# A two-layer hybrid decoder step: taps before each finish, no barrier behind the attention stream, row sums from the rows as loaded

## What is computed

```
h = x + W_out[ concat_g RMSNorm_g(mixer_g(RMSNorm(x))) ]
y = h + W2 relu(W1 RMSNorm(h))^2
```

```
def rmsnorm(x, g):
    xf = x.astype(jnp.float32)
    xf = xf * lax.rsqrt(jnp.mean(xf * xf, axis=-1, keepdims=True) + EPS)
    return xf.astype(x.dtype) * g

def merge_and_ffn(x, outs, p):
    B, T = x.shape[:2]
    o = jnp.concatenate([rmsnorm(o_i.reshape(B, T, GROUP_WIDTH), p['gnorm_g'][i])
                         for i, o_i in enumerate(outs)], axis=-1)
    h = x + o @ p['w_out']
    u = jax.nn.relu(rmsnorm(h, p['norm2_g']) @ p['w_ff1'])
    return h + jnp.square(u) @ p['w_ff2']
```

## Time and profile before

| | us |
|---|---|
| median of three runs | 3520.0 |
| the profiled execution, its own time | 3523.57 |
| its span, first to last instruction | 3521.8 |
| PE busy in it | 3298.5 (94%) |
| DVE busy | 1469.6 (42%) |
| ACT busy | 1017.1 (29%) |
| POOL busy | 203.7 (6%) |

### The profile page before, as it was taken

One profiled execution on the slowest core, in us unless ns is written; L12 is line 12 of the kernel. 1 busy time (PEld: TensorE's weight loads), 2 busy tenths in 40 slices (PEclk: granted clock), 3 DMA queues, 4 the chain that ended last, 5 costly groups with the idle time before them and its releaser, 6 DMA issues.

```text
span 3521.8 us, 55523 instructions
## 1 busy us (share of the span) xinstructions
PE 3298.5 (94%) x22450; PEld 1882.3 (53%) x22450; DVE 1469.6 (42%) x2767; ACT 1017.1 (29%) x1805; POOL 203.7 (6%) x136
## 2 busy tenths in 40 slices
PE   7999989888699999999999998888887999999998
PEld 4555466666444444444445555666664444444444
DVE  6865643333544311332178556433336533113322
ACT  2123344443433300231012232444443322012211
POOL 0211200000200000000011111000001000000000
PEclk9999999999899999999999998999998999999999
DMA  8323324323121211113163225234323112111222
GB/s 268 109 89 103 120 84 145 120 89 117 50 87 49 65 48 30 48 54 91 49 167 100 87 77 156 107 91 140 123 61 104 43 47 66 48 30 48 78 74 88
DMA packets 377028, 312.50 MB, mean 89 GB/s; under 512 B 122893, under 2 KB 359978, under 8 KB 369706
## 3 DMA queue, kind: packets, MB, share of 16 engines
q1 hardware_dynamic: 369402, 208.60, 21.0%
q0 software_dynamic: 7424, 101.19, 7.7%
HBM read 264.34 MB, written 50.46 MB: 89 GB/s over the span
## 4 chain that ended last, share of the span: by engine, by line
PE 86%; DVE 6%; ACT 4%; issue 2%; DMA 1%; SPq 1%; POOL 0%; POOLq 0%; DVEq 0%; ACTq 0%
PE PS L903 44%; PE PS L1018 11%; PE PS L1278 5%; PE PS L1301 5%; PE PS L932 4%; PE PS L1169 3%; PE PS L993 2%; PE PS L1320 1%; ACT arena L1583 1%; PE PS L1351 1%; PE PS L1215 1%; PE PS L1176 1%; DVE arena L2147 1%; DVE arena L1869 1%; PE PS L1068 1%
## 5 line engine op out<-in xcount | busy, mean ns | idle before, releaser
L903 PE MATMUL PS<-arena 128*128 128x512 bf16 (+1 forms) x10080 | 1549.1, 317 | 0.0
L903 PEld LDWEIGHTS PS<-arena 128*128 128x128 bf16 x10080 | 753.4, 98 | 794.7
L1018 PE MATMUL PS<-arena 128*128 128x512 f32 (+3 forms) x1152 | 477.6, 570 | 0.0
L1460 ACT ACTIVATE arena<-arena 128x1024 bf16<-128x1024 f32 (+1 forms) x112 | 145.4, 1300 | 1097.3 <-PE PS L903 1077.1
L2446 DVE TENSOR_TENSOR arena<-PS,arena 128x1088 f32<-128x1088 f32 (+1 forms) x48 | 62.0, 1291 | 654.8 <-PE PS L903 631.4
L1018 PEld LDWEIGHTS PS<-arena 128*128 128x128 f32 (+1 forms) x1152 | 208.3, 184 | 236.6 <-issue 203.6
L2152 DVE TENSOR_REDUCE arena<-PS 128x1 f32<-128x1024 f32 (+5 forms) x192 | 138.7, 723 | 372.4 <-PE PS L1281 371.7
L1278 PE MATMUL PS<-arena 128*128 128x512 f32 (+3 forms) x576 | 237.3, 520 | 8.0 <-ACT arena L1592 8.0
L2470 DVE SCALAR_TENSOR_TENSOR arena<-PS,arena 128x1088 f32<-128x1088 f32 x64 | 82.6, 1291 | 354.8 <-PE PS L903 354.3
L1301 PE MATMUL PS<-arena 128*128 128x64 f32 x1632 | 217.6, 280 | 0.0
L1301 PEld LDWEIGHTS PS<-arena 128*128 128x128 f32 x1632 | 205.1, 198 | 8.4 <-issue 5.4
(11 more groups left out here) (339 smaller groups left out, 2862.6 us busy)
## 6 DMA issues: line engine op xcount, KB each, us to landing
arena<-in_w_ff SPq DMA_DIRECT2D x64, 512.0 KB, 4.1
arena<-in_w_ff SPq DMA_DIRECT2D x32, 1024.0 KB, 5.9
arena<-in_cache_nsa_kv SPq DMA_DIRECT2D x256, 64.0 KB
x_s<-arena SPq DMA_DIRECT2D x24, 544.0 KB, 3.5
arena<-x_s SPq DMA_DIRECT2D x2, 4352.0 KB, 12.9
arena<-in_w_in SPq DMA_DIRECT2D x4, 2048.0 KB, 15.0
arena<-in_w_out SPq DMA_DIRECT2D x16, 512.0 KB, 4.3
arena<-in_w_in SPq DMA_DIRECT2D x12, 512.0 KB, 5.8
```

What stands on the lines that cost most here:

```text
L903: last = mm(PS[:, 1536 * k + a:1536 * k + a + wd], ww[:, c, :], xx[:, c, a:a + wd], start=c == 0 and n == 0, stop=c == blocks - 1 and n == 2)
L1018: last = mm(PS[0:r, c * 512:c * 512 + b - a], XNT[:, j, t * P:t * P + r], Wt[:, j, a:b], start=j == 0, stop=j == KD - 1)
L1460: run(WH[k][:, 0:blocks, :], src[k][:, 0:blocks, :], ACT.Copy).then_inc(S["w_hi"], 1)
```

## The change

Five things change.

1. **Start.** Rows are loaded in six DMAs ahead of the constants. ACT squares the rows as they are loaded, with the row on the partition, 896 of the 1024 channels, with a running sum; DVE copies the transposed rows to `XT` and puts each tile's sums on a diagonal of `SQA`, which the sum over partitions reads as well. The page tables come in 13 DMAs instead of 21, behind the first half of the gate weights.
2. **Last channels.** The squares of the last 128 channels (block 7) are taken after the barrier, at the next layer's beginning, both in the first layer and between layers. The sum over partitions moves from the head of the gated unit to its fifth channel block.
3. **Projection.** The taps stand ahead of `finish(t)`.
4. **Stream's tail.** For row tiles 2, 3 and 4 (`EARLY`), whose last head is complete first, the group norm, the transposes and the two bf16 halves go into the last five units of the stream as six more groups on the two banks. The sums of squares start two units earlier. ACT rounds the first two weight blocks and the convolution's channels in units 91 to 94, POOL subtracts their low halves.
5. **No barrier** between stream and merge. PE multiplies the columns of tiles 2 to 4 first, then those of 0 and 1, then the rest.

```diff
+        SUMMED = [(2, t) for t in range(QT + 1)] + [(g, t) for t in (2, 3, 4, 0, 1, 5, 6, 7) for g in range(2)]
+        SUM_FROM, SUM_EACH = LAST - 4, 3
+        EARLY, LATE = (2, 3, 4), (0, 1, 5, 6, 7, QT)
+        EARLY_ROWS = ((2 * P, 2 * P), (4 * P, P))
+        FIRST_ROWS, LAST_ROWS = ((0, 2 * P),), ((5 * P, 3 * P), (SEQ, NS))
...
-            here += {LAST + 1: [("ms",)], LAST + 2: [("ee",), ("gc",)], LAST + 3: [("wt",)], LAST + 4: [("mw",)],
-                     LAST + 5: [("mo", 0)], LAST + 6: [("mo", 1)], LAST + 7: [("mo", 2)]}.get(u, [])
+            here += {LAST + 1: [("ms",)], LAST + 2: [("ee",), ("gc",), ("hs",)], LAST + 3: [("wt",), ("gn", 2)],
+                     LAST + 4: [("mw",), ("oa", 2, 0), ("oa", 2, 1)], LAST + 5: [("mo", 0), ("mo", 1), ("gn", 3), ("gn", 4)],
+                     LAST + 6: [("mo", 2), ("oa", 3, 0), ("oa", 3, 1)], LAST + 7: [("oa", 4, 0), ("oa", 4, 1)]}.get(u, [])
...
@@ PE, head of the layer
-                sum_squares(SQA)
...
                             if f == 0 and s == 0:
                                 pe.wait_ge(S["xn_ready"], k + 1)
+                                if k == KD // 2:
+                                    pe.wait_ge(S["sq_added"], 1)
+                                    sum_squares(SQA)
...
@@ PE, behind the stream
-                arrive(pe, "pe")
...
+                pe.wait_ge(S["y_lo"], 2)
...
                 for n in range(2):
                     pe.wait_ge(S["w_lo"], n + 3)
-                    if n == 0:
-                        pe.wait_ge(S["oa_ev"], QT // 2)
-                    out_columns(n, STARTS[0], WIDTHS[0], {3: 6, 6: 7} if n == 0 else {1: 8})
-                pe.wait_ge(S["oa_ev"], QT + 1)
+                    if n == 1:
+                        pe.wait_ge(S["o_done"], NU // 8)
+                    out_columns(n, EARLY_ROWS, {4: 0, 6: 1} if n else None)
+                oa_T(2)
+                pe.wait_ge(S["oa_ev"], 2)
                 for n in range(2):
-                    for a, wd in zip(STARTS[1:], WIDTHS[1:]):
-                        last = out_columns(n, a, wd)
-                    last.then_inc(S["g_mm"], 1)
+                    out_columns(n, FIRST_ROWS, {5: 5} if n else {1: 3, 5: 4})
+                pe.wait_ge(S["oa_ev"], len(LATE))
+                for n in range(2):
+                    out_columns(n, LAST_ROWS).then_inc(S["g_mm"], 1)
...
@@ DVE, z_step
-                    finish(t, k)
                     for half in taps_of(t, 2):
                         conv(half)
+                    finish(t, k)
...
@@ DVE, start
+            for t in range(QT + 1):
+                r = rows_of(t)
+                dve.wait_ge(S["row_T"], t + 1)
+                for g in range(2):
+                    at = (2 * (t % 4) + g) * 512
+                    last = V.tensor_copy(XT[:, 4 * g:4 * g + 4, cols(t)], PS[:, at:at + 512].rearrange("p (j n) -> p j n", j=4)[:, :, 0:r])
+                last.then_inc(S["row_ev"], 1)
+                dve.wait_ge(S["sq_ready"], t + 1)
+                V.tensor_scalar(SQA[0:r, cols(t)], ident[0:r, 0:r], RSUM[0:r, t:t + 1], None, ALU.mult)
...
+            page_rows()
             arrive(dve, "dve")
...
@@ POOL, behind group D
-                everyone()
...
+                last_powers(EARLY[0], EARLY[-1] + 1, 1)
+                pool.sem_inc(S["w_lo"], 2)
+                for k in range(2):
+                    pool.wait_ge(S["w_hi"], k + 1)
+                    G.tensor_tensor(WLO[k], WFO[k], WHO[k], ALU.subtract).then_inc(S["w_lo"], 1)
+                for c in range(2):
+                    pool.wait_ge(S["y_hi"], c + 1)
+                    G.tensor_tensor(OTL[:, 2 + c, :], YB[:, c, :], OTH[:, 2 + c, :], ALU.subtract).then_inc(S["y_lo"], 1)
+                last_powers(0, 2, 2)
+                last_powers(5, QT, 3)
```

More of the change, by code:

```diff
@@ L212, in build_step @@
         SG, RST = SQ2[:, 0, :], SQ2[:, 1, :]
[L213 removed]
+        SQT = SQ2[:, 0, 0:DM - P]
         GV = g1.take(ROWS)
@@ L281, in build_step @@
         lo.at = after_xnt
[L282 to L285, removed]
+        OU = lo.take(24 * HD, u=24, d=HD)
+        ON = lo.take(QT * HD, t=QT, d=HD)
+        VF1 = lo.take(QT * HD, t=QT, d=HD)
         GH = lo.take(QT * 12, t=QT, c=12)
@@ L402, in build_step @@
         lo = Layout(arena, base, ARENA_W)
-        XS = [lo.take(DM) for _ in range(QT + 1)]
+        XSA = lo.take((QT + 1) * DM, t=QT + 1, n=DM)
+        XS = [XSA[:, t, :] for t in range(QT + 1)]
+        RSUM = lo.take(QT + 1)
         def sem(name):
@@ L593, in _ @@
             norm_in(first)
-            for f in range(2):
-                gates_in(f, first)
+            gates_in(0, first)
+            tables_in()
+            gates_in(1, first)
             def store_residual(n):
@@ L1110, in extra @@
                         merged(key)
+                    elif what == "oa":
+                        t = key[1]
+                        out = open_group(key)
+                        pe.wait_ge(S["od_norm"], 4)
+                        pe.wait_ge(S["oa_ready"], EARLY.index(t) + 1)
+                        for n, j in enumerate((2, 3, 4, 5) if key[2] == 0 else (0, 1)):
+                            last = tr(out[:, n * P:(n + 1) * P], OA[:, t, j // 2, (j % 2) * P:(j % 2 + 1) * P], ident)
+                        last.then_inc(S["pt_T"], 1)
                 def compressed(key):
@@ new lines, in _ @@
+                dve.wait_ge(S["h3_sq"], 2)
+                last_means(0, 2, len(SUMMED))
+                dve.wait_ge(S["h3_sq"], 3)
+                last_means(5, QT, len(SUMMED))
+                for i in range(2):
+                    group_norm(LATE[i])
+                for i in range(len(LATE)):
+                    if i == 2:
+                        dve.wait_ge(S["ss_ready"], len(SUMMED) + 2)
+                        V.tensor_scalar(S3[0:NS, 0:2, QT], S3[0:NS, 0:2, QT], EPS, None, ALU.add).then_inc(S["row_mean"], 1)
+                    if i + 2 < len(LATE):
+                        group_norm(LATE[i + 2])
+                    low(i)
```

373 lines of the change are left out of this document (197 added, 176 removed).

## The result

The changed kernel takes 3501.3 us as the median of six runs (3487.2 to 3504.2), beside 3518.6 for the kernel before: ratio 0.994, 95% interval 0.992 to 0.9961. That is a gain of 17 us by the medians and 21 by the ratio (14 to 28) where 46 were forecast, and the time lies 4 us above the range. The profiled execution took 3503.4 us (span 3501.3), so in the traces the gain is 20.

The account below looks back on a forecast made before the run. PE, busy 94% of the span, was taken as the bound. Start 5.0, projection 17.0, merge less tail 19.2 and layer's end 4.7 sum to 45.9 us: 3523.6 to 3477.7, 3474 beside the median; range 3456 to 3497.

Parts of the forecast that it names:

- the new end is therefore the tables' landing: Start: the page tables' landing, taken at 22.5 us, decides when PE begins; first product at 26.1, minus 5.0 us.
- The lower bound: Start: the tables land at 18 us at the earliest, if the small transfers slip past the gate weights.
- The rest of that step: Start, after the landing: page rows 1.5 us, barrier 1.3, then PE's first product after DVE's first product, 0.7.
- Projection: Taps ahead of finish remove PE's waits for ACT and the low clock behind them: 8.5 us a layer, 17.0 in all.
- The rival without the gain: Projection: something else, such as ACT's work, stands where DVE's stood, so the taps gain nothing; 3491 us, chance 0.12.
- Merge: Stream's end to third output block: the x reload sets the end, 33.2 us with low clock instead of 48.3, minus 15.1 a layer.
- The low clock behind the reload: Merge: after standing 5 us for the reload, PE pays 1.5 us of low clock.
- I take 5.5: Stream's tail: six added groups for the early transposes cost 5.5 us a layer, taken below 9 if all were serial.
- the lock: Stream's tail: DVE norms with two SBUF inputs and POOL's subtractions exclude each other; 3 x 1.2 us, inside the 5.5.
- a stage costed at nothing: Stream up to the last request's product, both layers: no change, 0 us.
- Layer's end: Last addition and the square before it go behind the barrier: 2.45 us each layer, 4.9 less 0.2 in all.
- The rival that the tail gives the merge back: Stream's tail: groups, lock and ACT's longer list are serial, 14 us a layer instead of 5.5; 3491 us, chance 0.15.

Follow-up runs that it names:

- 2: The changed kernel with the page-table DMAs issued ahead of the norm gains and the first gate weights: 3491.8 us, ratio 0.9916 to the kernel before.
- 5: The changed kernel with the 13 page-table DMAs issued by ACT instead of SP: 3494.8 us, ratio 0.992 to the kernel before.
- number 1: The kernel before with only the projection's taps put ahead of a tile's finish: 3512.6 us, ratio 0.9974.
- number 7: The changed kernel with a tile's finish put ahead of its taps again: 3516.2 us, ratio 0.9977 to the kernel before.
- 9: The changed kernel with a request's exponentials one unit sooner and finish ahead of the taps again: 3512.9 us, ratio 0.9975 to the kernel before.
- number 3: The changed kernel with the reload of x behind the merge's transposes made in two DMAs: 3484.6 us, ratio 0.9896 to the kernel before.
- Number 12: The changed kernel with POOL's four subtractions in the stream's tail cut to 32 columns: 3497.1 us, ratio 0.9931 to the kernel before.
- number 4: The changed kernel with the group norms of early tiles 3 and 4 one unit sooner: 3493.7 us, ratio 0.9914 to the kernel before.
- 6: The changed kernel with tables issued by ACT, reload in two parts and norms one unit sooner, together: 3472.5 us, ratio 0.9854 to the kernel before.
- 11: The changed kernel run again without an edit, giving its second trace: 3500.5 us, ratio 0.9938 to the kernel before.

## Why the prediction missed

**Start: the step "the new end is therefore the tables' landing", 22.5 us, failed.** The reasoning bounded the landing by bytes in the DMA engines and never asked when SP would issue. SP was held for 14.85 us in the two DMAs ahead, the tables were issued from 20.6 to 29.0 and landed at 30.7. The sign was in the earlier trace rows: SP took 10.62 us for 16 tables there and was done with them at 21.0, and in that trace single ones took 0.30 to 1.29 us. The lower bound was misread as well. The rate falls at 18 us, but in the same trace the requests' rows, issued at 6.0, landed 14.3 us later, and in the changed kernel DVE still waited for the constants until 21.25. The rest of that step (page rows 1.5, barrier 1.3, first product 0.8 behind DVE's) came nearly as written: 1.6, 1.4 and 0.9. Numbers 2 and 5 settle the cause. 8.5 us. Whether bytes or pieces fill the queue, no run separates.

**Projection: right.** 8.5 a layer forecast, 9.4 and 9.1 in the trace, 9.2 and 9.1 with that edit alone. The rival without the gain is out as far as the stage goes. Of these 16 to 18 us some 12, with 3 either way, reach the end of the kernel in the mean of three comparisons (numbers 1, 7, 9). Where the rest goes is open: the streams of number 1's trace are 6.9 us longer than those of before, 6.2 of it low clock, but number 7's clock losses did not fall when the taps went back.

**Merge: right in mechanism, and nearly in size.** 31.7 us to the third block forecast, 32.2 measured in the first merge and 34.1 to 34.3 in the other three of the two traces, with the reload as its end; number 3 shows it by removing it. In those three the merge begins at the low clock that the tail left: its first 72 products take 8.0 to 8.2 us instead of 6.1. The first 32.2 is thus the lucky case. The low clock behind the reload was mis-sized too: 1.5 forecast, 1.6 to 3.0.

**Tail: the term "I take 5.5" was mis-sized.** 5.5 a layer forecast, 5.9 and 10.8 measured, 8.8 and 10.7 in the second trace. Split by PE's busy time and clock from the last request's product to the last values, the mean of the kernel before's two tails and the range of these four:

| tail of the stream, us | before | changed, four tails |
|---|---|---|
| PE idle | 5.4 | 9.2 to 9.6 |
| lost to the low clock, (1 - clock) x time | 2.6 | 3.4 to 6.7 |
| the rest, work at full clock | 27.7 | 29.6 |

The forecast's 5.5 holds for work and waits together (1.9 and 3.9). It left out the low clock, which stands beside the added waits and costs 3.2 us a layer more than before in the mean. It is not tied to them one to one: the first tail has nearly the waits of the others and half their loss, and in numbers 2, 3, 5 and 7, where nothing in the tail is edited, it takes 42.6 to 47.2 us with 3.4 to 9.5 us lost to the clock and 8.8 to 9.7 us idle. The waits of PE, first in the tail before (898 to 945 us), then in the second one changed (2624 to 2672):

```profile
PE PS L1278 <- ACT arena L1592: 1.7, 1, 1.7
PE PS L1237 <- DVE arena L2147: 1.3, 1, 1.3
PE PS L1233 <- DVE arena L2147: 1.2, 1, 1.2
```

```profile
PE PS L1268 <- DVE arena L2200: 1.8, 1, 1.8
PE PS L1306 <- ACT arena L1616: 1.6, 1, 1.6
PE PS L1265 <- DVE arena L2200: 1.6, 1, 1.6
PE PS L1137 <- DVE arena L2400: 1.3, 1, 1.3
...
PE PS L1348 <- DVE arena L2411: 1.1, 1, 1.1
```

Two of them, for `L2400` and `L2411`, are new: one is a wait of the early transposes (`L1137`), the other one for the copies of the early halves. Number 12 shows that the lock is not what made the tail long, and number 4 that the place of the norms is 1 to 1.5 us a layer of the idle time. No run takes the early groups out of the tail, so that they are the cause is read from the waits and not tested.

**Stream: a stage costed at nothing moved by 3 to 9.5 us.** In eleven traces in which the stream is unedited (before, changed, and numbers 1 to 7, 11 and 12), each with two layers, the stage takes 495.7 to 509.5 us. PE's idle time in it is 63.4 to 66.9 and the work at full clock 416.7 to 419.0; the losses to the low clock are 13.7 to 25.6 and carry the spread. The mean is 502.1 us in the first layer and 504.6 in the second, so the profile of the kernel before, with 499.9 and 502.7, was 4 us on the lucky side in these stages, and the changed kernel's first trace 5 us on the other. What makes the clock fall behind one of these waits and not behind another is open.

**Layer's end: as forecast within a microsecond,** once the reload's gap is out of the way. From the third block to the next first product the changed kernel is 1.5 and 0.0 us slower where -0.9 was forecast, because of the low clock behind the gap. In number 3, without gap and low clock, the stage is 1.6 us shorter than before, and the last one of the kernel 2.7, where 2.45 each were forecast for the layer's end alone.

Added up over the first trace: start 8.5, stream 9.5, tails 5.7, merge and layer's ends 5.0, less 1.7 that the projection gave beyond its forecast: 27.0. Over the second: 8.9, 3.1, 8.5, 5.5, less 2.0: 24.0. My range was too narrow because each of its ends was one rival alone, while two terms and the chance of the clock failed together on the same side. The rival that the tail gives the merge back had the right place, and a third to a half of its 17 us came.

## What to carry to other kernels

A DMA's place is paid at its issue: before counting bytes, look at how long the issuing engine is held when megabytes already stand in its queue, and issue small urgent transfers from another engine. Price every wait that a change leaves on the tensor engine, or adds to it, with the low clock behind it; here that raised a 4.9 us wait to 6.5 to 8. And where a stage without an edit varies by 14 us from trace to trace, split it into idle time, low clock and the rest before explaining a shift in it.

## What the runs showed of the hardware

- Behind 4.5 MB of rows and 1.8 MB of constants SP took 14.85 us to issue two DMAs of gate weights (512 KB each), and 12.35 us for eight page tables (0.5 KB each) that took 5.10 us once that work was through. While SP was held, ACT's issues took 0.56 us each.
- The reload of x (128 rows of 34.8 KB) landed 13.0 us behind its issue; in two parts it no longer delayed the third block.
- Behind the same wait of 1.48 us, in an otherwise busy stretch, the granted clock fell from 2.4 to 1.2 GHz in one trace and stayed at 2.4 in another. One and the same program takes 3487 to 3504 us, with mean clocks of 0.982 to 0.976.
- POOL's subtractions with a bf16 result took 2.12 us (128x1024) and 2.25 us (128x1088), as estimated.
